# Third attention of a two-block transformer kernel: scores from split operands in three passes, query and key parts made on GpSimd

## The reference

```python
q = (rms_norm_2(c_q, mla_q_norm[j]) @ mla_w_uq[j]).reshape(b, s, N_TOK_HEADS, QK_DIM)     # 12 heads of 96
q = jnp.concatenate([q[..., :QK_NOPE], apply_rope(q[..., QK_NOPE:], positions)], axis=-1)  # 64 plain, 32 rotated
kv = (rms_norm_2(c_kv, mla_kv_norm[j]) @ mla_w_ukv[j]).reshape(b, s, N_TOK_HEADS, QK_NOPE + V_DIM)
k_nope, v = kv[..., :QK_NOPE], kv[..., QK_NOPE:]
k_rope = apply_rope(k_r[:, :, None, :], positions)
k = jnp.concatenate([k_nope, jnp.broadcast_to(k_rope, (b, s, N_TOK_HEADS, QK_ROPE))], axis=-1)
tok = causal_attention(q, k, v).reshape(b, s, TOK_WIDTH)
```

## Time and profile before

| | |
|---|---|
| median of three runs | 3132.32 us (3131.07 to 3132.60) |
| the profiled execution | 3131.1 us, its span 3129.0 us |
| PE busy | 3066.4 us, 98% of the span |
| DVE, ACT, POOL busy | 57%, 42%, 21% |
| chain that ended last | 90% PE |
| score matmuls of the third attention | 2418.8 to 2705.9 us |

### The profile page before, as it was taken

One profiled execution on the slowest core, in us unless ns is written; L12 is line 12 of the kernel. 1 busy time (PEld: TensorE's weight loads), 2 busy tenths in 40 slices (PEclk: granted clock), 3 DMA queues, 4 the chain that ended last, 5 costly groups with the idle time before them and its releaser, 6 DMA issues.

```text
span 3129.0 us, 50323 instructions
## 1 busy us (share of the span) xinstructions
PE 3066.4 (98%) x18600; PEld 2608.8 (83%) x18600; DVE 1791.4 (57%) x3573; ACT 1329.6 (42%) x2637; POOL 664.3 (21%) x886
## 2 busy tenths in 40 slices
PE   7999999999999999999999999998999999999999
PEld 7988888999999888888788888888977777787777
DVE  6657674353344322345888887876353666753675
ACT  5446565454445221232333333454433555522552
POOL 3423334453542000001111111001101011032240
PEclk9999999999999999999999999999999999999999
DMA  5110011011111321122233225643100000221012
GB/s 204 37 48 18 21 35 51 28 62 44 56 59 46 103 78 51 45 95 97 72 109 109 102 101 204 196 151 140 46 28 22 16 28 15 108 72 67 28 61 101
DMA packets 77412, 231.27 MB, mean 74 GB/s; under 512 B 17712, under 2 KB 21936, under 8 KB 65648
## 3 DMA queue, kind: packets, MB, share of 16 engines
q1 hardware_dynamic: 77168, 228.05, 20.8%
HBM read 183.92 MB, written 43.84 MB: 73 GB/s over the span
## 4 chain that ended last, share of the span: by engine, by line
PE 90%; DVE 6%; ACT 2%; issue 1%; DMA 1%; SPq 0%; POOL 0%; DVEq 0%; ACTq 0%; POOLq 0%
PE ps L2546 71%; PE ps L2589 7%; PE ps L2597 3%; PE ps L2553 2%; PE ps L2604 2%; PE ps L2620 2%; PE ps L2612 1%; PE ps L2623 1%; PE ps L2640 1%; DVE wlo L2815 0%; DVE hlo L2892 0%; ACT hhi L2660 0%; ACT whi L2650 0%; DVE qk L2923 0%; DMA fa2r<-scratch_fs 0%
## 5 line engine op out<-in xcount | busy, mean ns | idle before, releaser
L2546 PE MATMUL ps<-whi,hhi 128*128 128x256 f32 (+2 forms) x1920 | 580.5, 302 | 3.0 <-DVE hlo L2892 1.7
L2546 PE MATMUL ps<-whi,hlo 128*128 128x256 f32 (+2 forms) x1920 | 563.7, 294 | 0.0
L2546 PE MATMUL ps<-wlo,hhi 128*128 128x256 f32 (+2 forms) x1920 | 563.4, 293 | 0.0
L2546 PEld LDWEIGHTS ps<-whi,hhi 128*128 128x128 f32 x1920 | 368.2, 192 | 12.8 <-issue 5.1
L2546 PEld LDWEIGHTS ps<-wlo,hhi 128*128 128x128 f32 x1920 | 368.8, 192 | 7.4 <-issue 0.2
L2546 PEld LDWEIGHTS ps<-whi,hlo 128*128 128x128 f32 x1920 | 368.2, 192 | 7.7
L2546 PE MATMUL ps<-hhi,whi 128*128 128x512 f32 x864 | 342.3, 396 | 0.0
L2546 PE MATMUL ps<-hhi,wlo 128*128 128x512 f32 x864 | 337.0, 390 | 0.0
L2546 PE MATMUL ps<-hlo,whi 128*128 128x512 f32 x864 | 336.3, 389 | 0.0
L3154 POOL TENSOR_SCALAR stats<-stats 128x2 f32<-128x2 f32 (+2 forms) x230 | 59.3, 258 | 1194.1 <-ACT xsf L2654 509.1
L3143 POOL CAST whi<-raw 128x512 fp32r<-128x512 f32 (+4 forms) x180 | 113.7, 631 | 865.8 <-PE ps L2546 856.1
(11 more groups left out here) (616 smaller groups left out, 6996.6 us busy)
## 6 DMA issues: line engine op xcount, KB each, us to landing
raw<-in_W SPq DMA_DIRECT2D x61, 1024.0 KB, 4.8
scratch_fs<-fo SPq DMA_DIRECT2D x77, 256.0 KB, 2.0
raw<-in_W SPq DMA_DIRECT2D x24, 768.0 KB, 4.3
wd<-in_WD SPq DMA_DIRECT2D x44, 256.0 KB, 3.5
wf0b<-in_WF SPq DMA_DIRECT2D x10, 1024.0 KB, 5.3
wf1b<-in_WF SPq DMA_DIRECT2D x10, 1024.0 KB, 5.2
scratch_x<-x SPq DMA_DIRECT2D x16, 512.0 KB, 3.3
orw<-scratch_outs SPq DMA_DIRECT2D x6, 1024.0 KB, 5.8
```

The source lines that it names most:

```text
L2546: x = e.matmul(r.out, a, b, start=(r.start and m == 0), stop=(r.stop and m == n - 1), skip_group_check=r.joined)
```

## The change

All of it is in the third attention.

- Scores: queries and keys are kept as high and low parts (`mqh`, `mql`; `mkT000` and so on, whose last digit is 0 for the high part), and each piece is three matmuls: high x high, query high x key low, query low x key high. For `qt` = 4 the five key blocks are cut 2 + 3 instead of 4 + 1.
- Queries: ACT copies two transposed heads (96 x 256, plain) out of PSUM, POOL makes both parts. This is done per block row by `q_turn(n)`, called at the first unit of row n - 2, with three buffers; in the projection nothing is transposed any more. The rotation is done per half of the tokens, six operations of 128 columns.
- Keys: ACT copies both heads' half (128 x 512) to `raw1`, POOL makes both parts there, four transfers move them to `mkT`. The rotary rows go by ACT and POOL to one buffer pair and by six transfers to the others.
- Order: `proj(p)` is now key half, two query pieces, key half, values, two query pieces; the generator takes every second step for odd `p`. Inside the stage weight splits are not eager; from the fourth projection on loads are held, and after step 80 the second chunk of the output matrix is loaded and split.

```diff
+        mk_at = {(0, 0, 0): H + 12 * KB, (0, 1, 0): H + 16 * KB, (0, 0, 1): tails[0], (0, 1, 1): tails[1],
+                 (1, 0, 0): H + 20 * KB, (1, 1, 0): H + 24 * KB, (1, 0, 1): H + 28 * KB, (1, 1, 1): H + 32 * KB}
+        mkT = {key: at("mkT%d%d%d" % key, [T], R, o) for key, o in mk_at.items()}
+        mqT = [[inh("mqh0", [256], R, 36 * KB), inh("mql0", [256], R, 37 * KB)],
+               [inh("mqh1", [256], R, 62 * KB), rest("mql1", [256], R, 87 * KB)],
+               [inh("mqh2", [256], R, 9 * KB), inh("mql2", [256], R, 10 * KB)]]
+        mqs = [inh("mqs0", [256], F, 63 * KB)[:, :], col("kv_norm")]
+        mks = [raw[1][:, o:o + 512] for o in (1344, 832)]
+        krs = raw[0][64:96, 1344:1856]
...
+        def q_turn(n):
+
+            p, qt = n // 8, 7 - n % 8
+            q = Rec()
+            q.place, q.rotated, q.free = DB.take(), q_rotated[n // 4], flat(h_free, kr_places[1].full, q_used.get(n - 3))
+            q.src = [mq[:, mq_slot(n), s * 96:s * 96 + 96] for s in range(2)]
+            q.kept, q.before = mqs[n % 2][0:96, :], flat(h_free, q_read.get(n - 2))
+            q.hi, q.lo = [x[0:96, :] for x in mqT[n % 3]]
+            q.split = signal("mla_split")
+            emit("mq_turn", q)
+            q_read[n], q_turned[n] = q.split, q.place.full
...
+            def keys(hf):
                 cut = slice(hf * 512, hf * 512 + 512)
                 b = DB.take()
-                m = mm3(b, b.ps[:, :], views(ch.part(1), slice(0, 128)), views(cpair, cut), 2, ch.split)
-                evac(b, [(mkT[z_][s][0:64, cut], b.ps[64 * s:64 * s + 64, :]) for s in range(2)], set_q(p))
+                mm3(b, b.ps[:, :], views(ch.part(1), slice(0, 128)), views(cpair, cut), 2, ch.split)
+                k = Rec()
+                k.place, k.before, k.split = b, flat(h_free, k_moved), signal("mla_split")
+                emit("mk_out", k)
+                k_moved[:] = [load("mk", mkT[z_, s, x][0:64, cut].bitcast(F), mks[x][64 * s:64 * s + 64, :], k.split, set_q(p))
+                              for s in range(2) for x in range(2)][-1:]
+                p_fin[p] = list(k_moved)
                 yield
...
+            yield from keys(0)
+            yield from queries(0)
+            yield from keys(1)
             for t0 in range(0, 8 if p % 2 == 0 else 0, 2):
...
+            yield from queries(1)
+            if p == 3:
+                w_late[0] = 0
+            if p == 5:
+                p_last.append(q_rotated[11])
+            else:
+                ch.done(q_rotated[2 * p + 1])
...
+            kr_places.append([load("kr", mkT[z_, s, x][64:96, :].bitcast(F), mkT[0, 0, x][64:96, :].bitcast(F), kr_split, h_free)
+                              for z_, s in ((0, 1), (1, 0), (1, 1)) for x in range(2)][-1:])
...
+                    first = 2 if qt == 4 else 4
+                    for k0, n in ((0, min(first, qt + 1)), (first, qt + 1 - first)):
+                        if n > 0:
+                            pieces.append((tuple(x[0:96, 128 * s:128 * s + 128] for x in mqT[at_q % 3]),
+                                           tuple(mkT[z_, s, x][0:96, k0 * 128:(k0 + n) * 128] for x in range(2)),
+                                           tabM[:, 512 - n * 128:512] if k0 + n == qt + 1 else None))
...
+                    if s == 0 and at_q < 46:
+                        u.begin = lambda: q_next(at_q)
...
+        q_turn(0)
+        q_turn(1)
+        w_eager[0] = False
...
+            if i == 80:
+                w_eager[0], w_late[0] = True, None
+                raw_free[1], spl_free[1] = raw_free[1] + k_moved, [p_last[0], pairs[4][-1].s_full]
+                w_load()
+                w_split()
+                w_load()
...
+                        passes = ((0, 0), (0, 1), (1, 0)) if isinstance(r.parts[0].blocks[b][0], tuple) else (None,)
+                        for j in passes:
+                            for p in r.parts:
+                                q, k = p.blocks[b] if j is None else (p.blocks[b][0][j[0]], p.blocks[b][1][j[1]])
+                                x = e.matmul(p.place.ps[:, o:o + n], q, k, start=j == passes[0], stop=j == passes[-1])
...
-                    e.activation(r.dst, r.place.ps[0:96, :], ACT.Copy).then_inc(w.sig(r.place.read), 1)
+                    w.wait_each(r.before)
+                    e.activation(r.kept, r.place.ps[0:96, 0:256], ACT.Copy).then_inc(w.sig(r.place.read), 1)
+                elif kind == "mk_out":
+                    w.wait_ge(*w.last)
+                    w.wait_ge(*r.place.full)
+                    w.wait_each(r.before)
+                    e.activation(mks[1], r.place.ps[:, :], ACT.Copy).then_inc(w.sig(r.place.read), 1)
...
+            def split_kept(src, hi, lo, done):
+                w.wait_ge(*w.last)
+                e.tensor_copy(hi, src).then_inc(w.inner(), 1)
+                w.wait_ge(*w.last)
+                e.tensor_tensor(lo, src, hi.bitcast(F), ALU.subtract).then_inc(w.sig(done) if done else w.inner(), 1)
...
+                elif kind in ("kr_turn", "mq_turn"):
+                    w.wait_ge(*r.place.read)
+                    w.wait_each(r.free)
+                    split_kept(krs if kind == "kr_turn" else r.kept, r.hi, r.lo, r.split)
+                elif kind == "mk_out":
+                    w.wait_ge(*r.place.read)
+                    split_kept(mks[1], mks[0].bitcast(R), mks[1].bitcast(R), r.split)
```

More of the change, by code:

```diff
@@ L683, in scored @@
                         r.blocks = list(zip(q, rhs)) if isinstance(q, list) else [(q, rhs)]
-                        r.n = sum(k.shape[-1] for _, k in r.blocks)
+                        r.n = sum(width(k) for _, k in r.blocks)
                         r.out, r.mx = u.E[:, at_[x]:at_[x] + r.n], mxs[x][:, p:p + 1]
@@ L2165, in kr_turns @@
                 r.q0, r.place, r.free, r.rotated = q0, TB.take(), flat(h_free), kr_done
-                r.dsts = [mkT[0][s][64:96, q0 * 128:q0 * 128 + 512] for s in range(2)]
+                r.hi, r.lo = [mkT[0, 0, x][64:96, q0 * 128:q0 * 128 + 512] for x in range(2)]
+                r.before, r.split = list(kr_split), signal("mla_split")
                 emit("kr_turn", r)
+                kr_split[:] = [r.split]
                 yield r.place
@@ L2186, in proj @@
             cpair = (chi[:, 3:5, :], clo[:, 3:5, :])
-            for t0 in range(0, 8, 2):
-                b = DB.take()
-                for t in (t0, t0 + 1):
-                    mm3(b, b.ps[:, (t - t0) * 192:(t - t0) * 192 + 192], views(qpair, sl(t * 128, 128)),
-                        views(ch.part(0), slice(0, 192)), 3, ch.split, c_ready[0], last=t > t0)
-                q_read = evac(b, [(mq[:, t0:t0 + 2, :], b.ps[:, 0:384].rearrange("p (t c) -> p t c", t=2))], q_turned[0])
-                yield
@@ L2194, in proj, with queries @@
-            r = Rec()
-            r.read = q_read
-            emit("q_rotate", r)
-            for hf in range(2):
-                if hf:
-                    r.done = signal("q_rotated")
-                    emit("q_rotated", r)
+            def queries(half):
+                at_ = 4 * ((2 * p + half) % 3)
+                for j in (2, 0):
+                    t0 = 4 - 4 * half + j
+                    b = DB.take()
+                    for t in (t0, t0 + 1):
+                        mm3(b, b.ps[:, (t - t0) * 192:(t - t0) * 192 + 192], views(qpair, sl(t * 128, 128)),
+                            views(ch.part(0), slice(0, 192)), 3, ch.split, c_ready[0], last=t > t0)
+                    free = [q_turned.get(8 * p + 4 * half + n - 12) for n in range(4)]
+                    read = evac(b, [(mq[:, at_ + j:at_ + j + 2, :], b.ps[:, 0:384].rearrange("p (t c) -> p t c", t=2))], h_free, free)
+                    if j == 0:
+                        r = Rec()
+                        r.read, r.mq, r.t0, r.done = read, mq[:, at_:at_ + 4, :], t0, signal("q_rotated")
+                        q_rotated[2 * p + half] = r.done
+                        emit("q_rotate", r)
+                    yield
@@ L2266, in fills_m @@
             for p in range(1, 6):
-                for n in range(1 if p % 2 == 0 else 3):
+                yield
+                if p % 2 == 0:
                     yield
-                yield from proj(p)
-                for n in range(1 if p % 2 == 0 else 3):
+                for _ in proj(p):
+                    yield
+                    if p % 2:
+                        yield
+                for n in range(3 if p % 2 else 4):
                     yield
@@ L2586, in _ @@
                     for b in range(len(r.parts[0].blocks)):
-                        n = r.parts[0].blocks[b][1].shape[-1]
-                        for p in r.parts:
-                            x = e.matmul(p.place.ps[:, o:o + n], *p.blocks[b], start=True, stop=True)
-                            if b == len(p.blocks) - 1:
-                                x.then_inc(p.place.full[0], 1)
+                        n = width(r.parts[0].blocks[b][1])
```

(4 more changed lines are left out.)

71 lines of the change are left out of this document (30 added, 41 removed).

## The result

The changed kernel takes **3143.6 us** in the median (3139.57 to 3145.56), the kernel before 3130.76 on the same chip: ratio 1.0038, 95% interval 1.0028 to 1.0047. It is 0.4% slower, above the stated range (3118 to 3141).

What follows compares the result with a forecast made beforehand. PE was taken to bound the third attention. From 3131.1 us, -14.8 (scores) + 7.5 + 1.7 - 1.5 (opening) + 0.5 (output chunk) + 4.0 (rest of the stage) gave 3128.5 us, range 3118 to 3141.

Steps and rivals of the forecast that it cites:

- PE bounds the stage, so an instruction taken off it is worth its length: Third attention: PE busy 233.16 of 235.00 us, so cheaper scores gain their full 14.8 us unless something new makes PE wait.
- The price of the pieces: Scores: three passes cost 0.70, 0.53, 0.36, 0.33 us for 512, 384, 256, 128 keys; 78.1 us against 92.9 in fp32.
- The opening, +7.5 +1.7 -1.5: Stage opening: first scores late behind POOL's queue, 7.5 us lost; ACT held by key transfers, 1.7 lost; old waits gone, 1.5 gained.
- The second output chunk, +0.5: After step 80: loading and splitting the output matrix's second chunk takes 14.1 us against five steps of about 2.7; 0.5 us lost.
- The row chain and the port, +4.0: Rest of the stage: PE, ACT, POOL chain per block row, and POOL and DVE excluding each other on SBUF; 4 us lost.
- expected -10.3: Stage from the first scores on: the prediction's steps together made it 10.3 us shorter.
- the 13: Sign: the prediction is wrong if PE's waits on `mql` or on DVE sum to more than 13 us.
- The one on DVE: Rival, stage: DVE becomes the bound through the port shared with POOL; 3134.0 us, or 3143.5 at most; chance 0.15.
- Three passes are no cheaper here: Rival, scores: the gain of three passes is 0 and the losses stay; 3143 us; chance 0.02.
- The waits for GpSimd in every row: Rival, block rows: scores wait for GpSimd's query part in every row; 3139 us at 0.3 a row, 3148.5 at 0.5; chance 0.15.
- The covers hold: Rival: two-row lead covers every chain, POOL and DVE miss each other; 3121.8 us, or 3124.5 with the forecast's opening; chance 0.33.
- The chance of 0.23 for slower: Whole kernel: the chance given to the changed kernel being slower by over 0.2%.

Runs made afterwards that it cites:

- e5_fp32: Changed kernel with the scores as one fp32 matmul on the high parts again, low parts made but not used: 3151.95 us, 1.0068 of the kernel before.
- e14_last_fp32: `e13_last_pair` with one fp32 score matmul on the high parts in place of the three passes: 3130.58 us, 0.9998 of the kernel before.
- e13_last_pair: Changed kernel, opening's second key half later, two block rows turned early, rotation in three pairs (last pair's directly behind its queries), third chunk's split spread: 3123.07 us.
- e2_rot_late: Changed kernel with the six rotation operations of each query half put one filling step later in every queue: 3143.84 us, 1.0039 of the kernel before.
- e4_one_pass: Changed kernel with only one fp32r pass of the three left for the scores: 3129.30 us, 0.9994 of the kernel before.
- e6_pool_twice: Changed kernel with GpSimd making each of the 48 query parts twice over, same results: 3149.84 us, 1.0062 of the kernel before.

## Why the prediction was wrong, step by step

- **PE bounds the stage, so an instruction taken off it is worth its length.** This is the step that failed. It was read from 233.16 of 235.00 us busy, which only says that the helpers were fast enough for scores of 0.86 us. The spare time I looked at was DVE's sum; what counts is the time from a bank's fill to its release. The two score banks do stand in the prediction, but only as a way for longer DVE operations to reach PE (part of the 4.0), not as what shorter scores run into. Of 14.8 us, 8.4 arrive in the changed kernel (`e5_fp32`) and 7.5 in the well-ordered one (`e14_last_fp32`); of the 51 us of two passes left out, 14.3. The waits ahead of score pieces grew by 10.4 us in the stage (2.3 to 12.7).
- **The price of the pieces** was right. By the medians of the start distances, the three passes of 512 keys take 314, 231 and 232 ns, and the transpose ahead of them 28 instead of 109: 0.70 us net. Of 384 keys: 0.53, the middle that I took; of 256: 0.36; of 128: 0.29 in `e13_last_pair` (143, 113 and 112 ns) and 0.35 in the changed kernel, where the last distance holds a wait, against 0.33. My sum of the four products comes to 78.0, not 78.1, so the gain was 14.9 by its own terms; nothing hangs on it.
- **The opening, +7.5 +1.7 -1.5.** Measured +8.6. Mechanism and place were right, POOL's order included: the last query matmul ends at 2416.03 us and the first scores come 10.2 us later, where I had 10.0. The size is close partly by luck, since it is made otherwise: PE's idle time goes from 1.5 to 7.9 us (3.94, 2.02, 1.84), 3.2 us are half clock, and ten query transposes (1.1 us) have moved into the stage. That the first two block rows could have been turned before the last queries I did not see.
- **The second output chunk, +0.5.** No wait for it shows in the changed kernel. It appeared (2.1 us) only where the rotation was moved behind step 80.
- **The row chain and the port, +4.0.** The chain held: apart from the opening, PE never waits for GpSimd in the changed kernel. The port costs less than I feared: from 2400 to 2725 us the `mO<-stats` copies and the rotation run 8.7 us over their shortest lengths, 2.9 before, where I had 19 more; and in the fastest kernel, `e13_last_pair`, it is 11.0 us. What I left out is the rotation as one block of six ordered operations ahead of a bank's release, at rows whose step is shorter than the block; I had priced it as "6 us more" on an engine with 92 us idle. The count of such blocks doubled, from one per pair with its last two operations apart to two in one piece. Cutting and moving it gave 6.3 us.
- **The clock** was left out: 19.2 us of PE's work ran at half, which cost some 9.6 us. The Trainium skill ("TensorE: Matmul & The Clock Gate", "A second HAM failure mode: psum-queue depth-cycling") says of another kernel that short idle times of PE between groups of matmuls, frequent enough, brought the clock down again and again. The trace agrees: at 2630.42 us it fell behind waits of PE of 0.47, 0.23 and 0.52 us.

In numbers for the stage: expected -10.3, measured +5.3. Of the 15.6 between them, 4.8 are half clock, 5.3 are idle time beyond the 4.5 allowed, 1.1 are ten more of the query transposes that fall inside the stretch now; the other 4.4 lie within PE's busy time, mostly short waits that the modelled ends of matmuls cover (a transpose counts as 273 ns busy even where the score piece usually starts 28 ns behind it). The start distances bear this out: of the 12.7 us of waiting ahead of score pieces 5.8 show as idle, of the 2.3 before, 0.5, so 5.1 us more are covered.

**The signs I named.** Starts 0.23 us apart: right. A stall of 4 to 8 us at the first scores: 3.94, just under. `mO<-stats` and the rotation well over their best lengths: in the middle not (227 and 293 ns, their best); in the mean 316 ns for `mO<-stats` and 454 for the rotation's `cols<-mq,cs`. POOL busy 40% or more: 36% (100.39 of 280). PE idle under 12 us from 2420 to 2700: 16.5, the sign that spoke against the sum. PE's waits on `mql` and DVE: 3.9 + 4.6 + 4.1 + 2.0 + 1.7 = 16.3, over the 13.

**The rivals.** Closest in time are two, both by another mechanism than what happened. The one on DVE has 3143.5 at its far end through the port; the runs show order and bank release, with only 5.8 us more over the shortest lengths on DVE. "Three passes are no cheaper here" has 3143; `e5_fp32` and `e14_last_fp32` show that they are cheaper. The waits for GpSimd in every row did not come. "The covers hold" failed at the opening and the score banks. The chance of 0.23 for slower was too low because no case had shorter scores running into the bank release, nor the clock, which made the new waits dearer than their length.

What stays open: which part of DVE's and ACT's work on a score piece holds its bank longest, and where 2.3 of the 6.9 us that the passes still lose in `e13_last_pair` lie; neither engine was sped up by itself, and no run had more banks.

## What to carry to other kernels

A bound engine at 99% with two banks ahead of it is not free to run faster: before pricing what is taken off it, compare the shortest step's time with the chain that gives its bank back. Small operations on an engine with much idle time are better placed in pieces, at the long steps: as one block of 2.4 us at a short step they held the bound engine for up to 1.9 us here (`e2_rot_late`). And work that several queues pass on (weight splits, query parts) needs its order read on each queue at every place to which one of its inputs is moved, since a wait moved is a wait kept, until the order on the next queue is changed too.

## What the runs showed of the hardware

- At 2630.42 us waits of 0.47, 0.23 and 0.52 us were followed by 3.4 us at half clock (granted 0.50); in `e4_one_pass` with its many short waits this happened seven times in the stage. Each such stretch cost up to 1.7 us (an estimate: half of its length, where PE was at work throughout). In `e13_last_pair`, with 10 us of PE idle time spread over the stage, none appeared.
- Where fp32r passes follow an fp32 transpose, the transpose's distance to the next start shrinks from 109 to 28 ns, and the first pass's grows by 83 ns over the second (314 against 231): the change of kind costs next to nothing (83 against 81 ns), but a table of one group alone would misprice it.
- Three passes of 128 columns (0.29 us in `e13_last_pair`) are dearer than one fp32 matmul of them (0.22 us); with 256, 384 and 512 columns they are cheaper by 0.07, 0.11 and 0.16 us (0.36, 0.53 and 0.70 us against 0.43, 0.64 and 0.86).
- A DVE operation with both inputs in SBUF ran up to twice as long beside GpSimd (`e6_pool_twice`: 615 against 293 ns in the mean), while those that read PSUM kept their lengths (558 against 557 ns for 384 columns).
